# RWKV-7 chunk stage on one core: the chunk output taken out of `leave`, 64-row products first, and put behind the next level's products

## What is computed

```python
def step(S, inp):
    r_t, w_t, k_t, v_t, ma_t, b_t = inp
    sa = jnp.einsum('dbhij,dbhj->dbhi', S, ma_t)
    S = S * w_t[..., None, :] + sa[..., None] * b_t[..., None, :] + v_t[..., None] * k_t[..., None, :]
    return S, jnp.einsum('dbhij,dbhj->dbhi', S, r_t)
```

## Time and profile before

| what | value |
|---|---|
| time, median of 3 runs | 3148.43 us (3148.05 to 3151.59) |
| time of the profiled execution | 3147.97 us |
| its span | 3146.1 us |
| TensorE busy, matmuls | 2152.9 us (68%) |
| VectorE, ScalarE, GpSimd busy | 1269.3, 705.3, 664.4 us |
| mean granted TensorE clock | 0.820 |
| first chunk stage, 1024.80 to 1223.70 | TensorE busy 178.01 us, VectorE 54.86, ScalarE 68.65, GpSimd 49.80, clock 0.89 |
| last chunk stage, 2017.00 to 2217.00 | TensorE busy 174.18 us, VectorE 56.62, ScalarE 68.18, GpSimd 49.79, clock 0.91 |

### The profile page before, as it was taken

How to read it: one execution, slowest core, us unless ns; L and a number is a source line. 1 busy time by engine, 2 the same in 40 slices (tenths; PEclk the granted TensorE clock), 3 DMA queues, 4 the chain that set the end, 5 groups by cost and what they waited for, 6 DMA issues and landing times. The chain is left out here.

```text
span 3146.1 us, 50684 instructions
## 1 busy us (share of the span) xinstructions
PE 2152.9 (68%) x21252; PEld 1405.4 (45%) x21252; DVE 1269.3 (40%) x2416; ACT 705.3 (22%) x1436; POOL 664.4 (21%) x729
## 2 busy tenths in 40 slices
PE   7406412332465895669664985399389999999998
PEld 1203202322233784458543874287245555555553
DVE  0360588776505233343325322632233333332335
ACT  0210100110312332233212331243123222111121
POOL 0210523300220221022111211122242211111134
PEclk9658556666777896779776987699599999999999
DMA  7401000000100000000000000000242111110112
GB/s 264 174 28 34 3 5 8 8 1 8 33 28 1 3 3 4 23 3 3 3 24 2 2 3 25 2 2 3 102 143 105 54 54 54 54 48 7 54 52 96
DMA packets 62061, 119.74 MB, mean 38 GB/s; under 512 B 4358, under 2 KB 24326, under 8 KB 61578
## 3 DMA queue, kind: packets, MB, share of 16 engines
q1 hardware_dynamic: 61852, 116.65, 10.9%
HBM read 104.27 MB, written 10.27 MB: 36 GB/s over the span
## 5 line engine op out<-in xcount | busy, mean ns | idle before, releaser
L82 PE MATMUL psum<-arena 128*128 128x384 bf16 (+2 forms) x2244 | 741.7, 337 | 286.9 <-POOL arena L375 79.7
L83 PE MATMUL psum<-arena 128*128 128x384 bf16 (+2 forms) x2244 | 742.2, 337 | 0.0
L84 PE MATMUL psum<-arena 128*128 128x384 bf16 (+2 forms) x2244 | 739.5, 336 | 0.0
L82 PEld LDWEIGHTS psum<-arena 128*128 128x128 bf16 (+1 forms) x2244 | 225.2, 100 | 465.7 <-POOL arena L375 80.1
L1413 ACT ACTIVATE arena<-psum 128x256 f32<-128x256 f32 (+3 forms) x864 | 273.8, 328 | 525.7 <-PE psum L1335 179.4
L84 PEld LDWEIGHTS psum<-arena 128*128 128x128 bf16 (+1 forms) x2244 | 227.1, 101 | 172.7 <-issue 13.9
L83 PEld LDWEIGHTS psum<-arena 128*128 128x128 bf16 (+1 forms) x2244 | 226.5, 101 | 169.8 <-issue 11.9
L724 PE MATMUL psum<-arena 128*16 128x128 f32 (+1 forms) x128 | 29.1, 314 | 265.4 <-ACT arena L667 265.4
L2121 DVE TENSOR_TENSOR arena<-arena 128x384 f32<-128x384 f32 x96 | 103.1, 1074 | 236.6 <-ACT arena L1988 236.6
L1290 PE MATMUL psum<-arena 64*64 64x64 f32 x2880 | 180.2, 224 | 11.3 <-DVE arena L1584 11.3
L1289 PE MATMUL psum<-arena 64*64 64x64 f32 x2304 | 163.5, 233 | 9.6 <-DVE arena L1584 8.7
(11 more groups left out here) (280 smaller groups left out, 3309.1 us busy)
## 6 DMA issues: line engine op xcount, KB each, us to landing
arena<-in_w_ff SPq DMA_DIRECT2D x16, 2048.0 KB, 8.8
arena<-in_w_ada SPq DMA_DIRECT2D x12, 2048.0 KB, 7.9
arena<-in_x SPq DMA_DIRECT2D x18, 512.0 KB, 3.8
arena<-in_pos SPq DMA_DIRECT2D x18, 512.0 KB, 4.8
arena<-in_w_in SPq DMA_DIRECT2D x12, 512.0 KB, 4.1
x<-arena SPq DMA_DIRECT2D x9, 512.0 KB, 2.6
arena<-x SPq DMA_DIRECT2D x9, 512.0 KB, 3.3
out_y<-arena SPq DMA_DIRECT2D x9, 512.0 KB, 2.6
```

What stands on the lines that cost most here:

```text
L82: nc.tensor.matmul(out, whi, xhi, start=first, stop=False)
L83: nc.tensor.matmul(out, wlo, xhi, start=False, stop=False)
L84: return nc.tensor.matmul(out, whi, xlo, start=False, stop=last)
```

## The change

`leave` keeps the two products of the state update. The output becomes a function of its own, `output(g)`, with the two 64-row products first and the two 128-row products behind them, and is called one group of inverse products later: `output(g-1)` behind `begin`, `output(g)` behind `merge_q` of level 2, `output(g+1)` behind `merge_x` of level 3, `output(g+2)` behind `merge_q` of level 5, each straight ahead of an `enter`. ScalarE, VectorE and GpSimd have no change.

```diff
--- before.py
+++ after.py
@@ -1323,15 +1323,20 @@
             def leave(g):
 
                 d, s, tile, f, par, q = step_of(g)
-                x = R.x[d][:, tile]
                 pe.wait_ge(ev("u_read"), g + 1)
                 pe.wait_ge(ev("uv"), 2 * (g // 2) + 2)
                 pe.wait_ge(ev("tm"), g // 4 + 1)
                 for h in H2:
                     last = mm(PUT[half[h]], tm[par][q][:, f, half[h]], uv[par][q][:, f, half[h]], start=True, stop=True)
                 last.then_inc(ev("put"), 1)
+
+            def output(g):
+
+                d, s, tile, f, par, q = step_of(g)
+                x = R.x[d][:, tile]
                 for h in H2:
                     mm(MIX[half[f], h, mixcol(f)], slot(x, f, 1)[half[h]], state[g % 4][half[h]], start=True, stop=False)
+                for h in H2:
                     last = mm(MIX[half[f], h, mixcol(f)], mt[g // 2 % 6][:, h, f, f], uv[par][q][:, f, half[h]],
                               start=False, stop=True)
                 last.then_inc(ev("y"), 1)
@@ -1344,6 +1349,8 @@
                 if inv:
                     begin(i, 0)
                     begin(i, 1)
+                if i > 1:
+                    output(g - 1)
                 if old:
                     enter(g)
                 if inv:
@@ -1361,6 +1368,7 @@
                     merge_q(i, 2, 0)
                     merge_q(i, 2, 1)
                 if old:
+                    output(g)
                     enter(g + 1)
                 if inv:
                     merge_x(i, 2, 0)
@@ -1377,6 +1385,7 @@
                     merge_x(i, 3, 0)
                     merge_x(i, 3, 1)
                 if old:
+                    output(g + 1)
                     enter(g + 2)
                 if front:
                     score(2 * i + 2)
@@ -1396,6 +1405,7 @@
                     merge_q(i, 5, 0)
                     merge_q(i, 5, 1)
                 if old:
+                    output(g + 2)
                     enter(g + 3)
                 if inv:
                     merge_x(i, 5, 0)
@@ -1407,6 +1417,7 @@
             for i in range(PAIRS + 1):
                 body(i)
             leave(4 * PAIRS - 1)
+            output(4 * PAIRS - 1)
 
         @block.scalar
         def _(act):
```

## The result

The changed kernel takes 3122.02 us (median of 4 runs, 3119.90 to 3124.06); the kernel before, run again beside it, 3149.99 us. The ratio is 0.9911, 95% interval 0.9894 to 0.9929: 0.9% faster. The forecast was 3129 us, in a range of 3115 to 3147. The profiled executions, on which the sum was made, differ by 3147.97 - 3124.06 = 23.9 us.

The account below looks back on a forecast made before the run. TensorE was taken to bound the chunk stages, losing time to shape changes and waits for VectorE and ScalarE. From 3147.97 us, -8.9 for the bodies and -10 for the clock gave 3129 us, range 3115 to 3147.

Parts of the forecast that it names:

- The wait that takes the place: At `enter`, TensorE waits for ScalarE's `y_read` copy some 140 times instead of 16, each 0.4 to 0.5 us idle.
- rival D: `y_read` wait not met, TensorE's saving counts in full: 0.41 us a step, 59 us, to 3089 us; chance 0.07.
- The last body: Bare chain ending each chunk stage: `leave` to `enter` falls 0.41 us at full clock, 0.60 at half; 2.7 a stage.
- The clock: Eight chunk-stage bodies begin with a fall to half clock, 1.25 us each; expected to go, -10 us.
- rival B: Falls of the clock stay, since new waits at `enter` thin the stream as much: 3139 us; chance 0.20.
- A: As a stretch: `leave(g-1)` to `merge_x` 1, 3.08 us before, 3.20 after, +0.12.
- B: As a stretch: `leave(g)` to `merge_x` 2, 2.14 us before, 2.10 after, -0.04.
- C: As a stretch: `leave(g+1)` to `merge_q` 4, 3.13 us before, 3.36 after, +0.23.
- D: As a stretch: `leave(g+2)` to `merge_x` 5, 3.01 us before, 2.75 after, -0.26.
- E: Stretch from `merge_x` 5 to `leave(g+3)`: 1.27 us before, 0.08 more after, an estimate between 0 and 0.15.
- The span given for A: Main forecast A, waits eat the body's saving and clock falls go: 3129 us, span 3120 to 3137; chance 0.58.
- C (more falls): Rival: new waits ahead of `enter` bring clock falls in every full body, 20 more, 25 us: 3164 us; chance 0.15.

## Why the prediction held, and where it was off

- **The wait that takes the place.** The y_read wait came in all 140 steps that have one, 0.45 us each, as read from the last body: 0.78 us from the last group to `enter`. Doubling the copy and putting the output back both show it on the path. This was the main step, and it is why a change that, by rival D's sum, saves TensorE 0.41 us a step is worth 0.13 us a step (18.1 over 144).
- **The last body.** Forecast 1.41 and 1.94 us from `leave` to `enter`, measured 1.43 and 1.96.
- **The clock.** Forecast -10 us, measured -8.8; a fall costs 1.15 us and not 1.25, since that body takes 19.12 us undisturbed and not 19.02. That the thin seam is the cause was an argument then, and is shown in part: putting the block back there brought seven falls, but pairing alone, with the output still at the seam, took all of them away, and doubling the copy brought two without the block. That all eight went was more than the argument could promise. The Trainium skill's rule that the clock falls over long idle gaps (TensorE: Matmul & The Clock Gate, HAM oscillation) gave rival B; by this case's traces shorter ones are enough: the longest idle of the first stage's bodies with a fall is 0.54 us before, and in the rows of the changed kernel, whose full bodies have no falls, it is 0.46.
- **The body, the term that was mis-sized.** The stretches, forecast and measured: A 3.20 and 3.15; B 2.10 and 1.95; C 3.36 and 3.26; D 2.75 and 2.55; E 1.35 and 1.50. Sum +0.13 us against the kernel before, measured -0.21 (19.02 to 18.81). What failed is "0.17 (`enter`, an estimate: four passes and the spacing of the first)" and the start of `output`. L1289 starts 0.02 us after L1310, between its passes; that is the 0.15 of B and 0.15 of D. And L1338 runs among the last passes of the group ahead of it, about 0.05 us in A and D and 0.10 in C. E went the other way: it is now the bare chain `enter`, VectorE, `solve`, ScalarE, `leave`, 1.51 us from 1085.24 to 1086.75, as long as in the last body of the kernel before (`enter` at 1206.23, the next `leave` at 1207.74); I had put E at 1.35. Over 28 bodies the 0.34 are 9.5 us, about the difference between 8.9 forecast and 18.1 measured. That the time came out inside the range owes something to width: the order's own gain was twice the forecast. The span given for A, 3120 to 3137, doesn't follow from its own bounds either: 3129 less 28 x 0.4 and more 28 x 0.17 is 3118 to 3134.
- **Rivals.** B (falls stay) and C (more falls) did not come. D, 59 us for TensorE's time in full, was wrong for this change and nearly right for half of it: with the pairs in place and no new wait the gain is 71 us (3150.92 to 3080.31), some 9 of it the clock's, if each of the eight falls is put at 1.15. The Trainium skill (TensorEngine Tiling (Array Packing), Key Properties) has the array drained at a change of tiling mode. These runs agree that a change costs time: with two of a step's six gone `leave` takes 0.90 us and not 1.29. The page gives no price, and says nothing of who waits next. The list had no rival in which the move itself was the costly part and the pairing alone the better kernel, though each of its numbers stood in the text.

## What to carry to other kernels

Before moving work away from a critical instruction, look at what waits for the moved work: an output right ahead of the instruction that needs its buffer read turns a saving into a wait, while one group between them (0.5 us here) hid the copy wherever it was kept. Order small matrix products by shape so that the group starts with the shape of the one before it and ends with the shape of the one after; the first two changes saved took 0.39 us off a step and the next two 0.22 (17.45 to 16.58 us a body), so each was worth four to seven passes of 0.03 us. Try the two parts of such a change apart, since here one alone was worth -71 us and the other alone +36, and both together only -28.

## What I had not expected of the hardware

- Products of neighbouring groups run between each other's passes: L1310 and L1289 start 0.02 us apart (1092.96 and 1092.98), and in the kernel with the 128-row products first L1337 and L1278 start 0.01 us apart (1102.13 and 1102.14). In the second case the pair isn't free, as shown above. That such products stand on different quarters of the array is read from the code; no run here tests it.
- TensorE starts 0.15 us after ScalarE's end at `enter` (ScalarE 1200.18 + 0.27 to 1200.60), but 0.06 us at `leave` (1198.84 + 0.27 to 1199.17). Both stand behind more than one wait in the code (`enter` two, `leave` three); what makes the difference was not tested.
